# Summing the squares of x on VectorE instead of GpSimd, with the statistic columns inside the fourth product

## What is computed

```python
h = x * rsqrt(mean(x * x, axis=-1) + 1e-6) * g
proj = h @ w_in            # or h @ w1, h @ w3, h @ w_up
...
x = x + rmsnorm(mix, g2)   # first block; the second block adds without this norm
```

## Time and profile before

| | |
|---|---|
| Median of three runs | 2632.11 us |
| The profiled execution | 2633.78 us, its span 2631.8 us |
| TensorE (PE) busy | 2476.9 us, 94% |
| VectorE (DVE) busy | 1491.4 us, 57% |
| ScalarE (ACT) busy | 1079.8 us, 41% |
| GpSimd (POOL) busy | 135.3 us, 5% |
| Mean granted TensorE clock | 0.961 of 2.4 GHz |

### The profile page before, as it was taken

One profiled execution on the slowest core, in us unless ns is written; L12 is line 12 of the kernel. 1 busy time (PEld: TensorE's weight loads), 2 busy tenths in 40 slices (PEclk: granted clock), 3 DMA queues, 4 the chain that ended last, 5 costly groups with the idle time before them and its releaser, 6 DMA issues.

```text
span 2631.8 us, 33085 instructions
## 1 busy us (share of the span) xinstructions
PE 2476.9 (94%) x11614; PEld 1990.9 (76%) x11614; DVE 1491.4 (57%) x2226; ACT 1079.8 (41%) x1421; POOL 135.3 (5%) x134
## 2 busy tenths in 40 slices
PE   7977989999889998999998989999999989999999
PEld 6755768888768876888886747788888757788887
DVE  6865455552367755555325565687733565587732
ACT  4334343332346553433323363454422463454421
POOL 2000110000010002000002000000001000000000
PEclk8888889999999998999998998999999998999999
DMA  6321123333322212333333201333333300333331
GB/s 148 82 63 32 41 64 104 96 92 96 100 56 72 74 54 64 106 98 98 90 96 96 71 9 33 88 104 96 93 97 104 89 25 9 91 109 96 92 97 67
DMA packets 401417, 209.79 MB, mean 80 GB/s; under 512 B 18052, under 2 KB 397592, under 8 KB 401336
## 3 DMA queue, kind: packets, MB, share of 16 engines
q1 hardware_dynamic: 397927, 199.70, 26.3%
q0 software_dynamic: 3408, 9.02, 1.4%
HBM read 204.49 MB, written 4.19 MB: 79 GB/s over the span
## 4 chain that ended last, share of the span: by engine, by line
PE 85%; DVE 8%; ACT 3%; issue 1%; DVEq 1%; POOL 0%; DMA 0%; ACTq 0%; SPq 0%; POOLq 0%
PE bank L603 65%; PE bank L639 8%; PE bank L1031 2%; DVE w_lo L1527 1%; ACT w_hi L1114 1%; PE bank L1056 1%; PE bank L1071 1%; DVEq L1556 1%; PE bank L666 1%; DVE tmp L1568 1%; DVE x L1636 1%; PE bank L855 1%; PE bank L816 0%; PE bank L991 0%; PE bank L700 0%
## 5 line engine op out<-in xcount | busy, mean ns | idle before, releaser
L1527 DVE TENSOR_TENSOR w_lo<-w_raw,w_hi 128x1024 fp32r<-128x1024 f32 x380 | 477.9, 1258 | 659.4 <-ACT w_hi L1114 655.1
L603 PE MATMUL bank<-h_hi,w_hi 128*128 128x512 f32 x1848 | 730.5, 395 | 10.2 <-DVE w_lo L1527 4.6
L603 PE MATMUL bank<-h_lo,w_hi 128*128 128x512 f32 x1848 | 721.7, 391 | 0.0
L603 PE MATMUL bank<-h_hi,w_lo 128*128 128x512 f32 x1848 | 721.2, 390 | 0.0
L1114 ACT ACTIVATE w_hi<-w_raw 128x1024 fp32r<-128x1024 f32 x380 | 401.2, 1057 | 639.9 <-PE bank L603 638.2
L603 PEld LDWEIGHTS bank<-h_hi,w_hi 128*128 128x128 f32 x1848 | 348.5, 189 | 89.0 <-issue 14.5
L603 PEld LDWEIGHTS bank<-h_hi,w_lo 128*128 128x128 f32 x1848 | 348.2, 188 | 73.4 <-issue 2.6
L603 PEld LDWEIGHTS bank<-h_lo,w_hi 128*128 128x128 f32 x1848 | 348.0, 188 | 73.1
L603 PE MATMUL bank<-hid_hi,w_hi 128*128 128x512 f32 x704 | 273.9, 389 | 0.0
L603 PE MATMUL bank<-hid_hi,w_lo 128*128 128x512 f32 x704 | 273.9, 389 | 0.0
L603 PE MATMUL bank<-hid_lo,w_hi 128*128 128x512 f32 x704 | 273.9, 389 | 0.0
(11 more groups left out here) (406 smaller groups left out, 2916.6 us busy)
## 6 DMA issues: line engine op xcount, KB each, us to landing
w_raw<-in_ffn_w SPq DMA_DIRECT2D x120, 512.0 KB, 3.8
w_raw<-in_w_up SPq DMA_DIRECT2D x88, 512.0 KB, 3.8
w_raw<-in_c_w_in SPq DMA_DIRECT2D x32, 512.0 KB, 4.1
w_raw<-in_w_down SPq DMA_DIRECT2D x32, 512.0 KB, 3.9
w_raw<-in_w_in SPq DMA_DIRECT2D x28, 512.0 KB, 3.9
w_raw<-in_w_o SPq DMA_DIRECT2D x16, 512.0 KB, 3.8
w_raw<-in_ab_w_in SPq DMA_DIRECT2D x12, 512.0 KB, 7.2
w_raw<-in_ffn_w SPq DMA_DIRECT2D x16, 384.0 KB, 3.4
```

The lines of the kernel that those rows point to most:

```text
L603: mm = nc.tensor.matmul(out[:], w[:, s, k], v[:, kt], start=(kt == 0 and w is w_hi and v is hi), stop=(kt == sum(slabs) - 1 and v is lo))
L1527: nc.vector.tensor_tensor(w_lo[:, s], w_raw[:, s], w_hi[:, s].bitcast(F32), ALU.subtract).then_inc(lo_done, 1)
```

## The change

At the four borders VectorE makes the six additions, behind its last h_lo. The columns of `sq_sum` and of the eighth square both move to the middle of the fourth product, and the spread moves from the middle of the fourth product to its end. GpSimd keeps the sums of `sq_mix` and `sq_ffn` and those of the other borders. The rest of the diff keeps the semaphore counts right.

```diff
-            for norms in ((sq_mix,), (sq_in, sq_ffn), (sq_in, sq_mix), (sq_in, sq_ffn), (sq_in,)):
-                for sq in norms:
-                    add_squares(sq)
+            for sq in (sq_mix, sq_ffn, sq_mix, sq_ffn):
+                add_squares(sq)
+                n(sq_ready, KD)
...
-            def enter(last_square):
-
-                group(h_hi, h_lo, before=(KD - 1, add_sum))
-                add_square(last_square)
-                product(h_hi, h_lo, [KD], 1, halfway=spread_inverse)
+            def enter(last_square, pooled=False):
+
+                def statistic():
+                    add_sum()
+                    add_square(last_square)
+
+                if pooled:
+                    group(h_hi, h_lo, before=(KD - 1, add_sum))
+                    add_square(last_square)
+                    product(h_hi, h_lo, [KD], 1, halfway=spread_inverse)
+                else:
+                    group(h_hi, h_lo)
+                    product(h_hi, h_lo, [KD], 1, halfway=statistic)
+                    spread_inverse()
...
             def gated(i):
-                enter(tmp[:, (KD - 1) % 4] if i else sq_in[:, KD - 1])
+                enter(tmp[:, (KD - 1) % 4] if i else sq_in[:, KD - 1], pooled=bool(i))
...
             def conv_ffn(i):
-                enter(sq_in[:, KD - 1])
+                enter(sq_in[:, KD - 1], pooled=True)
...
                 low(KD - 2)
                 settle(h_ready)
+                n(sq_ready, KD)
+                for k in range(1, KD - 1):
+                    dve.wait_ge(sq_ready, n(sq_ready, 2 if k == 1 else 1))
+                    add = nc.vector.tensor_tensor(sq_sum[:], sq_in[:, 0] if k == 1 else sq_sum[:], sq_in[:, k], ALU.add)
+                    if k < KD - 2:
+                        step(add)
+                        settle()
+                    else:
+                        add.then_inc(sum_ready, 1)
+                n(sq_ready, 1)
```

More of the change, by code:

```diff
@@ L1147, in load_root, with deviation @@
                 return nc.scalar.activation(warm[:], eps[:], ACT.Sqrt)
-            def deviation(width):
+            def deviation(width, pooled=True):
                 act.wait_ge(stat_ready, n(stat_ready))
-                if width == D:
+                if width == D and pooled:
                     n(pool_step, KD - 3)
@@ L1318, in enter @@
                     nc.scalar.activation(sq_in[:, k], x[:, k], ACT.Square).then_inc(sq_ready, 1)
-                deviation(D)
+                deviation(D, pooled=False)
             def ffn(i):
```

## The result

The changed kernel takes 2636.35 us in the median of 19 runs (2635.18 to 2646.55), the kernel before 2633.11 beside it (2631.47 to 2635.47, 19 runs). The ratio is 1.0018, 95% interval 1.0012 to 1.0025: 3.2 to 6.6 us slower, about the 0.2% that one can tell from no change. Forecast was +6.6 us with a range from 0 to +10.4. Beside other kernels later the ratio was 1.0016 (1.0007 to 1.0025).

What follows compares the result with a forecast made beforehand. PE, busy 94% of the span, was taken as the bound. Border shifts of +0.6 us plus +6.0 for the clock gave +6.6: 2640.4 us profiled, 2638.7 median; eight-in-ten range 2632 to 2642.5, the forecast's own 2635.5 to 2641.5.

Steps and rivals of the forecast that it cites:

- What goes: At the borders, DVE's collisions with POOL vanish; first h_lo comes 2.12 us earlier, PE starts the group at 346.02, not 348.14.
- What comes: Six additions on DVE behind its last h_lo, 5.4 us, hidden by 6.4 us of margin: zero, bounds 0 and +0.5.
- The bound beside the loads: In gated 0, six additions beside POOL's loads at 1.8 us each would end about 5.4 us later, still inside the margin.
- What moves on PE: Sixteen columns after half the fourth product end at 1.76 us; the statistic is complete at 369.61, 0.53 us later than before.
- What hangs on the statistic: Chain from statistic to free bank 0 moves +0.53; borders: ffn 0 and ffn 1 -0.27 each, c and gated 0 +0.55 each.
- What the new pause does to the clock: Half clock behind the pause before the fifth product, 2.0 us lost at ffn 0, ffn 1 and gated 0: +6.0; c costs nothing.
- the clock that holds: Rival: the clock stays up behind the new pauses at the borders, only +0.6 us is left, 2632.7; chance 0.20.
- the one that falls at a single border: Rival: the clock falls behind the pause at only one of three borders, +2.6 us, 2634.7; chance 0.10.
- The columns didn't lower the clock: Rival: columns, 1.8 us without a full matmul, slow the fourth product's second half too: +9 to +11, 2642; chance 0.06.
- The faster rival: The earlier start reaches the fifth product, which follows right behind the spread at two borders: -6 us, 2626; chance 0.05.

Runs made afterwards that it cites:

- pause_filled: The changed kernel plus unread matmuls in the pause before the fifth product, 7 at the ffn borders, 12 at c and gated 0: 2633.08 us, 1.0004 against the kernel before.
- additions_twice: The changed kernel with VectorE's six additions done twice over at each of the four borders: 2636.22 us, 1.0013 against the kernel before.
- adds_only: The changed kernel with columns and spread back in their places of the kernel before, VectorE still adding: 2628.18 us, 0.9983 against the kernel before.
- spread_at_end: The changed kernel with the columns back in their old places, the spread still behind the fourth product: 2636.49 us, 1.0013 against the kernel before.
- both_columns_early: The changed kernel with both sets of columns ahead of the group's last tile, spread in the middle of the fourth product: 2619.74 us, 0.9950 against the kernel before.

## Why the prediction came out

- **What goes** was right to the hundredth: the wait before the group is 6.34 us at all four borders, instead of 8.46 to 8.49; additions and h_lo at 0.69 and 0.75 each.
- **What comes**: right. The additions are hidden, even twice over. They took 4.3 us, not 5.4: they start 0.73 apart, so the 0.21 of idle between them was too much. The bound beside the loads had a slip: six at 1.8 with 0.21 each end 6.7 us later, not 5.4, which is over the margin of 6.4. In gated 0 they took 4.3 us as well, beside those loads.
- **What moves on PE**: right. Columns 1.70 us long in front of the next matmul (1.71 with the refill expected), pause of 3.92 from the fourth product's end to the fifth's start for 3.97. It splits into 1.33, the spread and 1.81.
- **What hangs on the statistic**: -0.27 at the ffn borders. In the profiles ffn 0 gave -0.74, but the half-clock stretch at the start of its group was 4.3 instead of 5.7 us, which at 0.47 per us is 0.7 of it. At c +0.55 was forecast and +1.15 seen, with that stretch 5.4 instead of 3.0 us (1.1 more) and a shorter one behind c's wait. In gated 0 -0.43 for +0.55, with 3.4 instead of 6.0. At ffn 1 -0.27 was forecast and +0.87 seen: the start has 2.9 instead of 4.8 us (0.9 less), the half clock behind the pause adds 1.6, and 0.4 is left over. In all, the starts have 16.0 instead of 19.5 us at half clock, which took back the 1.6 that the pause cost. I had taken these stretches as equal in both kernels; that they aren't moves single borders by up to 1.2 us either way. pause_filled, whose clock is undisturbed behind the four pauses, came out at +0.6 in the median (-1.3 to +3.4), and at -0.1 over the borders of its profile: the sum for everything but the pause's clock agrees with it, the tenth is luck.
- **What the new pause does to the clock** is the term mis-sized: "3 x 2.0 = +6.0". Filling the pause gave 2.6 to 4.1 us back, not all of it at the pause (above). In two profiles one border of three had the half clock, for 3.4 us of work (1.6 us lost), in the third two of three had it (in ffn 0 for 5.7 us of work, 2.7 lost, the upper bound; in gated 0 1.4 lost). I had it fall each time. The Trainium skill, "TensorE: Matmul & The Clock Gate", section "HAM oscillation — how this bites in real kernels", would have left the clock alone for gaps that are short singly, as all of these are; the half clock behind c's 3.17 us, behind ffn 1's 1.33 and 1.80 and, in one of three profiles, behind gated 0's 2.9 speaks against reading it so.
- **What had no term** is the code behind the borders. In the changed kernel's two profiles it lost 2.6 and 2.7 us, more than the clock right behind the pauses (1.6), and the starts of the groups gave about as much back. That the time still came out in the range is partly luck: two losses, one of them unforeseen, stand in for a term of 6.0 that was too large. The forecast's own range is too low by a slip, too: its bounds give +4.5 to +9.7, from 2636.6, where the text has 2635.5. The measured 2636.35 lies just below.
- Of the rivals, the clock that holds (+0.6) is what pause_filled built; the one that falls at a single border (+2.6) has the clock as two of three profiles show it. The columns didn't lower the clock in any profile. The faster rival is out: the fifth product waits for bank 0 at every border.

## What to carry to other kernels

When a step is moved behind work so that it no longer delays that work, follow what hangs on it to its end: here a whole chain over three engines (statistic, root, reciprocal, spread, free bank) was in order behind it, and 2.12 us gained at its head became a pause at its foot. Move the producer earlier and leave the consumer where its input comes, rather than the other way: the same additions with the columns ahead of the last tile are worth 13 us. In the profile 12.0 of the 13 are at the borders. And test a suspected clock loss by filling the pause with useless matmuls: the row behind the pause then tells what the clock cost there (1.6 us at ffn 1). The time of the whole kernel doesn't, as long as unchanged code behind can move by 2 to 3 us on its own.

## What the runs showed that was not expected

- Whether 8 or 16 matmuls of nothing are added makes 3.7 us of difference for 1.8 us of work; in the same piece of code the mean clock was 0.96, 0.93 or 0.86, and its length 45.5, 47.2 or 50.4 us. Differences of 0.1 to 0.2% between kernels can be of this kind. Executions differ in it too: behind the borders the changed kernel's two profiles have +2.6 and +2.7, that of additions_twice, the same to TensorE, has -1.2.
- Unchanged code behind the borders lost in the same places in five of the profiles (the changed kernel's two, adds_only's two, spread_at_end's): +1.0 to +1.2 us between 1500 and 1590, +0.6 to +0.8 between 1590 and 1650, +1.6 between 2050 and 2100. In all other profiles the last of these is -0.1 to 0.0. Why it goes one way or the other stays open.
- adds_only gains 9.1 and 9.6 us at its borders and 3 to 4 us in the median (2628.18 and 2629.44). Why its timing is an unlucky one, and that of both_columns_early isn't, stays open.
- A VectorE operation with two inputs in SBUF took up to 1.80 instead of 0.69 us beside an addition of GpSimd in the kernel before; in other meetings it took its usual time, and GpSimd's addition up to 1.75 instead of 1.31. One that reads a bank and one input in SBUF took 0.73 to 0.75 throughout, beside GpSimd too.
